# A pooling, sliding-window-attention and MLP block on eight cores: attention cut into 32 half blocks and set among the projections and gates

## What is computed

```
u = rms_norm(x, norm_mix);  z = u @ w_in          # 512 pool | 512 q | 128 k | 128 v | 1024 gate_pool | 1024 gate_attn
pool: per group g of 128 channels, trailing mean over 2, 4, 8 or 16 tokens minus the token,
      then a 128x128 linear map, a bias and a scale per channel
attention: 8 query heads of 64, 2 kv heads (query heads 0-3 use kv head 0, 4-7 kv head 1), window 128,
      ALiBi bias -slope*distance, one sink logit per head in the softmax's maximum and sum;
      in blocks of 128 queries against 256 keys (the block before and this one)
mixed = sigmoid(gate_pool) * (pool @ p_pool) + sigmoid(gate_attn) * (attn @ p_attn)
h = x + mixed @ w_out
h = h + relu(rms_norm(h, norm_mlp) @ w_up)**2 @ w_down       # inner width 4096
y = rms_norm(h, norm_final)
```

## Time and profile before

| | |
|---|---|
| median of 3 runs | 939.73 us (939.09 to 940.59) |
| the profiled execution, slowest of 8 cores (core 1) | span 939.2 us; the eight cores 935.4 to 939.2 us |
| mean granted TensorE clock | 0.944 of full speed on core 1; dies 0.943 and 0.942 |
| busy share of the span | PE 90%, weight loads 43%, DVE 42%, ACT 34%, POOL 22% |
| chain that ended last | PE 72%, ACT 8%, DVE 7%, issue 7%, DMA 3%, POOL 3% |
| 3840 matmuls made at L388 | 786.3 us busy, mean 370 ns |
| DMA | 55.92 MB moved, mean 60 GB/s |

### The profile page before, as it was taken

How to read it: one execution, slowest core, us unless ns; L and a number is a source line. 1 busy time by engine, 2 the same in 40 slices (tenths; PEclk the granted TensorE clock), 3 DMA queues, 4 the chain that set the end, 5 groups by cost and what they waited for, 6 DMA issues and landing times.

```text
span 939.2 us, 13818 instructions; the slowest of 8 cores (935.4 to 939.2 us)
## 1 busy us (share of the span) xinstructions
PE 848.6 (90%) x4441; PEld 401.8 (43%) x4441; DVE 392.4 (42%) x582; ACT 321.7 (34%) x678; POOL 207.8 (22%) x236
## 2 busy tenths in 40 slices
PE   1589966887999999999999999999999999999994
PEld 1344423444444444444444444444444444444441
DVE  2362189999222222236642233232222332224545
ACT  2263547999322222225542211112211112223322
POOL 3021722000124232221122111211112111113333
PEclk9999985655799999999999999999999999999998
DMA  9860019400005050069707400560008300001213
GB/s 174 159 180 25 2 13 142 72 2 1 1 1 68 1 68 1 1 144 231 165 23 109 72 1 0 85 96 1 1 1 126 54 1 1 1 1 68 90 67 135
DMA packets 37398, 55.92 MB, mean 60 GB/s; under 512 B 6992, under 2 KB 21584, under 8 KB 37328
## 3 DMA queue, kind: packets, MB, share of 16 engines
q0 software_dynamic: 28816, 27.95, 21.2%
q1 hardware_dynamic: 8512, 27.09, 9.0%
HBM read 74.04 MB, written 8.39 MB: 88 GB/s over the span
## 4 chain that ended last, share of the span: by engine, by line
PE 72%; ACT 8%; DVE 7%; issue 7%; DMA 3%; POOL 3%; DVEq 0%; POOLq 0%; ACTq 0%
PE psum L388 69%; ACT arena L399 6%; DVE arena L403 5%; DMA arena<-w_in 3%; PE psum L392 3%; POOL arena L403 2%; ACT arena L418 2%; DVE arena L408 1%; DVE arena L413 0%; POOL arena L423 0%; DVE arena L662 0%; DVEq L194 0%; POOLq L280 0%; ACTq L194 0%; DVE arena L716 0%
## 5 line engine op out<-in xcount | busy, mean ns | idle before, releaser
L388 PE MATMUL psum<-arena 128*128 128x512 bf16 (+3 forms) x3840 | 786.3, 370 | 29.3 <-DMA arena<-w_in 17.6
L388 PEld LDWEIGHTS psum<-arena 128*128 128x128 bf16 (+1 forms) x3840 | 361.4, 101 | 436.0 <-issue 43.5
L403 POOL TENSOR_TENSOR arena<-arena 128x512 bf16<-128x512 f32 (+3 forms) x199 | 179.6, 909 | 686.4 <-ACT arena L399 291.3
L399 ACT ACTIVATE arena<-psum 128x512 f32<-128x512 f32 (+1 forms) x208 | 124.1, 598 | 450.7 <-PE psum L388 447.6
L403 DVE TENSOR_TENSOR arena<-psum,arena 128x512 f32<-128x512 f32 (+2 forms) x241 | 177.4, 761 | 155.5 <-PE psum L388 122.0
L399 ACT ACTIVATE arena<-arena 128x256 bf16<-128x256 f32 (+2 forms) x209 | 137.4, 685 | 110.3 <-DVE arena L403 49.2
L403 DVE TENSOR_TENSOR arena<-arena 128x512 bf16<-128x512 f32 (+5 forms) x93 | 58.0, 624 | 155.9 <-ACT arena L399 152.5
L392 PE MATMUL psum<-arena 128*128 128x128 bf16 x601 | 75.1, 260 | 48.3 <-DVE arena L408 18.0
L413 DVE SCALAR_TENSOR_TENSOR arena<-arena,psum 128x512 f32<-128x512 f32 x64 | 43.9, 688 | 124.9 <-PE psum L388 121.8
L392 PEld LDWEIGHTS psum<-arena 128*128 128x128 bf16 x601 | 43.5, 110 | 87.9 <-issue 87.5
L418 ACT COPY arena<-psum 128x1024 bf16<-128x1024 bf16 (+4 forms) x57 | 43.7, 818 | 21.5 <-PE psum L388 21.5
(11 more groups left out here) (13 smaller groups left out, 14.4 us busy)
## 6 DMA issues: line engine op xcount, KB each, us to landing
arena<-x SPq DMA_DIRECT2D x32, 512.0 KB, 7.4
arena<-w_up POOLq DMA_DIRECT2D x4, 2048.0 KB, 17.7
arena<-w_down POOLq DMA_DIRECT2D x4, 2048.0 KB, 22.9
y<-arena SPq DMA_DIRECT2D x16, 512.0 KB, 2.7
arena<-w_in POOLq DMA_DIRECT2D x9, 512.0 KB, 10.6
arena<-w_out POOLq DMA_DIRECT2D x1, 2048.0 KB, 31.9
arena<-w_in POOLq DMA_DIRECT2D x4, 256.0 KB, 18.2
arena<-w_in POOLq DMA_DIRECT2D x1, 1024.0 KB, 31.3
```

The costliest lines, as they stand in the source:

```text
L388: P.op("pe", lambda e: e.matmul(out, lhsT, rhs, start=start, stop=stop), r=[lhsT, rhs], w=[out])
L399: return e.activation(out, in_, func, bias=bias, scale=scale, **kw)
L403: P.op(eng, lambda e: e.tensor_tensor(out, in0, in1, op), r=[in0, in1], w=[out])
```

## The change

The program keeps `Prog`, the helpers and the MLP. What differs:

- **Schedule.** Operations are no longer made in the order of loops. Each is entered with `at(t, ...)` at a planned time in us, and the list is sorted by that time before it is recorded. The planned times are constants in the code. By them the first projection stands at 21.4, the first half block at 36.8, the first gate at 110.7 (by then 10 half blocks have begun, 8.1 apart, the last two 6.15 apart), the last half block ends at 254.1 and the last gate at 301.6.
- **Projections** chunk by chunk: for each of the 4 pieces of 512 tokens K, V, 4 q and 4 pool slices. V is computed directly in its final layout (32 matmuls of 128 columns a piece). The halo tile comes fifth and serves K, V and the last 16 tokens of each pool group only.
- **Pooling** per piece of 512 tokens, all window sums on POOL, the last 16 columns carried over by a POOL copy.
- **Attention** in 32 half blocks of 4 heads: the host permutes the queries (and p_attn and the sinks), so that a matmul's 64 rows always match K's halves; `ks_swap` is gone. The bias table is bf16; one DVE addition of 1024 columns reads both score banks. The sink is written by a DVE copy into score column 0 (which the window masks). The probabilities are divided before the transposes, on DVE. V is the stationary operand, so the output comes out transposed and needs no PE transpose; ACT copies it.
- **PSUM.** A ring of 4 banks for projections and gates, 2 banks for scores, 1 for transposes, 1 for outputs.
- **Weights.** The host lays out w_in, p_pool and p_attn so that a partition reads 4 KB or 2 KB runs. All gate and mix weights stay resident (48 KB a partition), loaded in four steps at planned times 26, 44, 62 and 80. Eight small constants become one table.
- **Order of gates:** all 8 slices for one piece of tokens, then the next; the result overwrites the normed input.
- **w_out stage:** transposes two tiles behind; x tiles for `HT` are loaded as soon as attention has ended; the last two tiles' transposes stand inside the first MLP piece.

```diff
-        eng = "pool" if g < 3 else "dve"
...
-            tt(eng, nxt[:, lo:2176], cur[:, lo:2176], cur[:, lo - sh:2176 - sh], ALU.add)
+            tt("pool", nxt[:, lo:528], cur[:, lo:528], cur[:, lo - sh:528 - sh], ALU.add)
...
+        stt("dve", d_t, cur[:, 16:528], 1.0 / w, up[:, 16:528], ALU.mult, ALU.subtract)
...
+        if s < 3:
+            cp("pool", up[:, 0:16], up[:, 512:528])
...
+    def att_s(i):
+        b, j = i // 2, i % 2
+        for ci in range(2):
+            for g in range(2):
+                mm(bank(4 + g)[:, ci * 256:(ci + 1) * 256],
+                   QT[g * 64:(g + 1) * 64, 2 * j + ci, b * 128:(b + 1) * 128],
+                   KT[g * 64:(g + 1) * 64, b * 128:b * 128 + 256])
+
+    def att_bias(i):
...
+        tt("dve", asb.rearrange("p h k -> p (h k)"), psum[:, 4 * 512:6 * 512], bt[:, j, :], ALU.add)
+        cp("dve", asb[:, :, 0], SINK[:, 4 * j:4 * j + 4])
...
+        P.op("dve", lambda e: e.tensor_reduce(nm, asb, AX.X, ALU.max, negate=True), r=[asb], w=[nm])
+
+    def att_exp(i):
...
+        for h in range(4):
+            act(asb[:, h, :], asb[:, h, :], AF.Exp, bias=nm[:, h:h + 1], accum=rs[:, h:h + 1])
+
+    def att_norm(i):
...
+        P.op("dve", lambda e: e.reciprocal(rd, rs), r=[rs], w=[rd])
+        for h in range(4):
+            ts("dve", apn[:, h, 1:256], asb[:, h, 1:256], rd[:, h:h + 1], None, ALU.mult)
...
+    def att_ptevac(i):
...
+        cp("act", APT[i % 2], pt)
+
+    def att_pv(i):
...
+        for kc in range(2):
+            for g in range(2):
+                mm(bank(7)[g * 64:(g + 1) * 64, 0:256], V[:, b + kc, g * 64:(g + 1) * 64],
+                   apt[:, g, kc, :], start=(kc == 0), stop=(kc == 1))
+
+    def att_oevac(i):
...
+        cp("act", QT[:, 2 * j:2 * j + 2, b * 128:(b + 1) * 128],
+           bank(7)[:, 0:256].rearrange("p (c k) -> p c k", c=2))
+
+    def half_block(t, i):
+        at(t, att_s, i)
+        at(t + 0.6, att_bias, i)
+        at(t + 3.2, att_exp, i)
+        at(t + 5.7, att_norm, i)
+        at(t + 8.2, att_tr, i)
+        at(t + 8.9, att_ptevac, i)
+        at(t + 12.0, att_pv, i)
+        at(t + 12.7, att_oevac, i)
+        return t + 13.0
...
+        at(t, gate, WGP)
+        at(t + 1.73, mix, WPP, PMT)
+        at(t + 1.80, lambda: act(tg[0], box[0], AF.Tanh, scale=0.5))
+        at(t + 2.60, gate, WGA)
+        at(t + 2.70, lambda: stt("dve", tg[0], tg[0], 1.0, box[1], ALU.add, ALU.mult))
+        at(t + 4.33, mix, WPA, QT)
...
+    dma("pool", IDENT, ident_d, "ident")
+    w_load(0, 1)
+    w_load(1, 2)
+    x_load(1)
+    dma("sp", CST, cst_d, "cst")
+    x_load(2)
+    x_load(3)
...
+    for n, c in enumerate(range(2, 6)):
+        at(2.0 + n, w_load, c, c + 1)
+    at(8.0, w_load, 6, 8)
+    at(11.0, w_load, 8, 10)
...
+    for n, m in enumerate(range(0, 8, 2)):
+        at(26.0 + 18 * n, g_load, m)
...
+        if t >= 2:
+            f_tr(t - 2)
+        if t >= 1:
+            f_scale(t - 1)
+        rs_f[t] = norm_stats(HT[t], t)
```

More of the change, by code:

```diff
@@ L358, in _build @@
+    RL = [sb(UTX0 + 36864 + 2048 * i, 512, F32) for i in range(2)]
     STG = []
-    for base in (PMT0, MIX0):
+    for base in (WG0, QT0):
         STG.append(dict(
@@ new lines, in _build @@
+    for u in seq:
+        d = u(t)
+        if isinstance(d, tuple):
+            t_att = t + 1.2
+        else:
+            t += d * F_B
+    t_g = t
+    d_b = (t_g - 9.0 - t_att) / 8
+    ta = t_att
+    t_end = 0.0
+    GL = 5.19 * 1.15
+    for i in range(32):
+        t_end = half_block(ta, i)
+        ta += d_b if i < 7 else 6.15
+    if DEBUG:
+        print("t_att", t_att, "t_g", t_g, "d_b", d_b, "t_end", t_end, "g3", t_g + 24 * GL)
+    for s in range(4):
+        for m in range(8):
+            g_unit(t, s, m)
+            t += GL
+            if s == 0 and m < 4:
+                pl_unit(t - 0.3, 3, m)
@@ L814, in mlp_up @@
             tt("pool" if fc % 2 else "dve", a2[:, fc, :], rl, rl, ALU.mult)
+            if mid is not None:
+                mid(fc)
     pending = []
```

789 lines of the change are left out of this document (337 added, 452 removed).

## The result

The changed kernel takes 900.55 us (median) against 939.88 us for the kernel before, measured in turn on one chip. The ratio is 0.9574, 95% interval 0.956 to 0.9588: 4.3% faster. Two of the six executions of the changed kernel and one of the six of the kernel before came out at 986 to 1034 us with one half of the chip at a lower clock; medians in this document are over all executions, ratios leave such ones out, and without them the two medians here would be 899.75 and 939.73 us. The forecast was 859.6 us, its range 832 to 900. So the direction was right, the gain half of what was forecast (39 us instead of 80), and the result lies 0.55 us above the range.

A forecast was written before the change was run, and what follows sets the result against it. PE bounds gates and MLP; elementwise work bounds attention, DMA the start. Start 26 + projections 105.4 + gates 206.5 + w_out 79 + MLP and tail 442.2 = 859.1, median 859.6 us; range 832 to 900.

The forecast's parts named there:

- w_out: w_out with first MLP piece: 79 us (ends 76.5 and 89.6) against 89.6 before, transposes no longer waiting for ACT.
- the gates: Gates with 23 half blocks: 202.5 us of PE work plus 4 for waits, 206.5 us, ends 187 and 240.
- the term for waits in the projections: Projections: 10% added to PE's 95.9 us for queue waits, 9.5 us, ends 0 and 25, giving 105.4.
- The sign that the prediction named for being wrong: PE waiting for DVE's epsilon or scale behind POOL for over 20 us would show the forecast wrong.
- a price for POOL's powers: POOL's power step beside a DVE step with two SBUF operands took 1.57 us instead of 0.55, through the shared port pair.
- coupling: Rival: in projections POOL, or DVE and ACT in turn, become the bound, powers behind window sums; 885 to 905 us, chance 0.19.
- Its case against: Against coupling: the power is needed only once per 5 us, and half of DVE's work has one SBUF operand.
- The full price for changes of form: Each half block: four changes between matmul forms lose 0.17 us each, 0.68 on top of 0.87, giving 1.55 us.
- 2%, 4 us: Gates: allowance for waits added to 202.5 us, as PE stays the longest engine.
- Slower than before: Rival: interleaved stages keep the clock at 1.2 GHz, each wide matmul costing 0.216 us more; up to 1088 us, chance 0.04.
- Cheaper attention: Rival: no loss at changes of form and few waits in half blocks; 831 us, chance 0.13.
- The schedule doesn't overlap: Rival: no way seen except half blocks missing each piece's last mix; 10 us each costs 40, inside the coupling case.

The follow-up runs named there:

- Experiment 8: All 32 half blocks left out (attention not computed), on the kernel of experiment 2: 823.37 us, ratio 0.8745.
- experiment 5: Changed kernel with the 32 half blocks alone between projections and gates, planned 4.6 us apart: 1016.6 us, ratio 1.0809.
- Experiment 4: Changed kernel with scaling and transposes of w_out one tile behind again, as in the kernel before: 908.89 us, ratio 0.965.
- Experiment 3: Changed kernel with the four gate weight load steps planned 34 us later: 900.86 us, ratio 0.9567.
- experiment 1: Changed kernel with all 40 window sums on POOL left out (pooling not computed): 866.68 us, ratio 0.9197.
- experiment 2: Changed kernel with each window sum planned 1.15 us after the one before, DVE's step 0.2 us after the last: 882.70 us, ratio 0.9369.
- experiment 9: Changed kernel, sums still made and bunched, but DVE's pool step reads the token instead (pooling not computed): 886.27 us, ratio 0.9414.
- experiment 10: POOL's powers of the first norm left out (norm not computed), on the kernel of experiment 2: 880.13 us, ratio 0.9343.
- 13: All window sums on DVE instead of POOL, on the kernel of experiment 11: 877.60 us, ratio 0.9328.
- experiment 11: Kernel of experiment 2 with pool slices spread over pieces, plus half blocks from the ninth locked to gate units (5.97 us apart): 877.03 us, ratio 0.9313.

## Why the prediction was right, and where it was wrong

**Right: what the gain is made of.** The stage of 102.7 us at a clock of 0.58 and the stall ahead of it were to vanish into stages whose engines had room. They did, but with far less gain than forecast. Projections and gates together took 354.0 us, where before projections, attention and gates took 370.0 (from 40.5 us to the first w_out matmul at 410.5; the gates' row ends 3.1 us early). So the interleaving brought 16.0 of the 41.6 us between the two profiled spans, where the forecast had 366.9 - 311.9 = 55; the earlier start brought 15.0 and w_out 10.5. Experiment 8 prices what is left of attention at 59 us, and experiment 5 shows that without the interleaving the same operations, in this order, cost 116 us more.

**Right: start, w_out, MLP.** The first full-width projection came at 25.5 us (forecast 26). From the first w_out matmul to PE's last, 410.5 to 926.0 before, it was 515.5 us; now, 379.5 to 884.5, it is 505.0. That is 10.5 less. The forecast had 89.6 - 79 = 10.6, but from a row that begins 3.1 us before w_out: with 429.0 for the rest of the MLP the stage took 86.5 before and 76.0 now, 3 less than the 79 forecast, which is the -3.1 of the table. Experiment 4 gives 8.3 of it to the transposes two tiles behind. Experiment 3 shows that the loads of gate weights were hidden or nearly so, as taken.

**Wrong: the term for waits in the projections.** PE's work was put at 95.9 us with 9.5 for waits, 25 as the worst. Without window sums (experiment 1) the stage takes 111.0 us, 5.6 over the forecast of 105.4: PE is busy 99.4 and idle 11.6. So the rest of this stage's sum was right to 6 us. The engines' work was about right too, DVE 82.8 us for 80, ACT 73.0 for 79, POOL 56.9 for 70. The failed step is the one that concluded from such shares that waits add 10%, 9.5 us, and let POOL's 40 sums pass as 37 us of work on an engine with room. The sums cost 25.1 us there. The sign that the prediction named for being wrong, PE waiting over 20 us for the scale, came: 23.0 us. The sums act in two ways:

1. *A wait written into the order*, which no part and no rival of the prediction has. In the diff `pool_ops` makes up to four sums and DVE's step at one planned time. The sums last 1.1 us each, so DVE stands up to 5 us before its step, and with it the scale, the transposes and PE. Giving the sums their time moved the projections from 136.1 to 122.2 us and the gates from 217.9 to 215.2, 18 us in all (experiment 2); taking DVE's wait away gave 14 (experiment 9). This could have been read from the diff and the earlier trace rows: 10 sums of 0.93 us a piece against zero planned.
2. *POOL and DVE hold each other up.* The prediction saw and took it as a price for POOL's powers. It works on DVE too, and the sums are the large load. That DVE's operations get longer is shown; what it costs is not shown by itself. From experiment 2 to 1 there are 16 us, 11.2 of them in the projections (122.2 - 111.0), and from 9 to 1 there are 20, with no wait for the sums on DVE. Powers behind sums in POOL's queue have some 3 of them at most (experiment 10). With the sums on DVE, where divisions and scales aren't lengthened but DVE has more to do, the time is the same (13). How much of the 16 us the 6.1 us of waits left in experiment 2 make was not tested. In its section Who interferes with whom the page SBUF — State Buffer of the Trainium skill says that DVE's instructions with two SBUF inputs meet POOL's reads, that scaling and copying may too in their fast modes, and that reductions and those with one SBUF input outside these modes don't. The runs agree on each kind: two SBUF inputs 682 to 970 ns (experiments 1 and 9), scale 750 to 1130 (1 and 2), addition from PSUM and reduction 1217 to 1221 in all of them. That the later one is blocked for a whole instruction these means can't tell.

Both gave PE gaps, and the granted clock was 0.84 at 36 to 110 us (0.95 there without sums). The rival "coupling" gave 885 to 905 us and had a chance of 0.19. It had the end of the chain right: the scale is late and PE waits for transposes. But it put powers behind the sums at the start of it, with POOL as the bound, and powers were worth some 3 us in the kernel of experiment 2, and POOL was busy 56.9 of 136.1 us. So that 900.55 lies in its range is in part luck. Its case against, that half of DVE's work has one SBUF operand, doesn't say where it counts the divisions and scales; they have one SBUF operand too and do lengthen.

**Wrong by less: the gates.** 217.9 us instead of 206.5. Without sums they take 210.1, so 7.8 of the 11.4 go with the sums, those of the last piece and what they leave behind: PE is busy 16.3 of the first 23.4 us, at a clock of 0.78. In the middle of the stage the timeline of PE shows a half block with a unit without a wait, and later with one:

```profile
223.55 0.61 PE L339 MATMUL psum<-arena 128*128 128x128 bf16 x8
...
230.05 0.61 PE L339 MATMUL psum<-arena 128*128 128x128 bf16 x8
...
252.14 1.05 PE L339 MATMUL psum<-arena 128*128 128x128 bf16 x8 [0.52 <-DVE arena L355]
...
259.71 1.18 PE L339 MATMUL psum<-arena 128*128 128x128 bf16 x8 [0.55 <-DVE arena L355]
```

Without a wait the period is 6.50 us, with it 7.57. Take 24 wide matmuls at 0.2158 us, 5.18, from 6.50, and a half block costs PE 1.32 us where 1.55 was forecast. V's pairs run together (experiment 5), so the columns need 0.87. The full price for changes of form, 0.68 us by four overlaps of 0.17, is too high: 1.32 - 0.87 = 0.45 is left. The rule of the Trainium skill (TensorEngine Tiling (Array Packing), section Key Properties) that a change of tiling mode drains TensorE isn't refuted by this, but the step by which it gave 1.55 is. So the sum here had an error of 23 x 0.23 = 5 us in its favour, and "2%, 4 us" for waits was really some 20 (217.9 less 202.5 - 5). Part of it may be the drift between 6.15 and 5.97 us: locking the two gave 5.4 us in the gates but 2.7 in all, against 8 to 11 expected (experiment 11).

**The rivals.** "Slower than before" by the clock was seen only in small: 0.84 for 74 us and 0.78 for 23, where that rival had 0.50 for whole stages. "Cheaper attention" was partly right on the loss at changes of form (0.45 us a half block, not 0.68, and not 0) and wrong on few waits. "The schedule doesn't overlap" saw no way for waits but the last mixes; the sums planned at one instant with their reader were one.

**What stays open.** With the phase locked PE meets the divisions still running, which would explain 0.45 of the 0.52 us between 7.02 and 6.50; this is read from the timeline, and no run moved DVE's divisions to test it. The 12 us of waits in the projections without sums were not taken apart (most are still transposes that wait for the scale). How the 16 us between experiments 2 and 1 divide into longer DVE work, waits that are left and a lower clock was not separated, and no run keeps DVE's work and takes the meeting away. Whether this form of attention set among the other stages beats the old form alone but with the other parts of the change was not run either.

## What to carry to other kernels

When an order is written by planned times, a consumer on another engine must be planned after the producer's whole duration: here the in-order queue turned a plan of zero for 4 us of work into 4 us for everything behind it. POOL and DVE aren't two separate stores of free time: add up for DVE what POOL's large two-input operations add to its scales, divisions and steps with two SBUF inputs, and try the sums on either engine before you count one as free. Busy shares don't show the waits that an order makes: here DVE was busy 61% of the projections and POOL 42%, and PE waited all the same. And put a price on waits from a stage that already interleaves several engines, not from a percentage.

## What the runs showed of the hardware that was not expected

- Beside POOL's additions of some 520 f32 columns DVE's scale of 1024 columns took 1.13 us on average instead of 0.75 and the division of 255 columns 0.52 instead of 0.35 (experiment 2 against 1, at 45 to 136 us), the step with two SBUF operands 0.97 instead of 0.68 (9 against 1), and a copy of 4 columns 0.41 instead of 0.17 (11 against 1). Additions of 1024 columns with a PSUM operand and reductions of 1024 kept 1.22 us in each of these runs.
- POOL's sum of 527 columns took 1.12 us on average in the kernel after. By length the 3.81 us for 2175 columns would give 0.93:

```profile
L350 POOL TENSOR_TENSOR arena<-arena 128x527 f32<-128x527 f32 x15 | 16.9, 1125 | 25.7 <-ACT arena L365 17.7 <-DVE arena L360 3.0 <-ACT arena L346 1.9
```

- Moving 24 us of sums from POOL to DVE left the time as it was (experiments 11 and 13).
- Four matmuls of 128 rows, 64 output partitions and 256 columns on alternating column halves took 0.64 us at a granted clock of 0.50 (experiment 5), less than the 0.85 of one after the other.
